# Paged attention in a decoder step: K and V pages laid on 64 partitions, and score and V products of 128 columns instead of 64

## What is computed

```python
k_past = cache_k[page_table].reshape(Bd, P, H, hd)
v_past = cache_v[page_table].reshape(Bd, P, H, hd)
s_past = jnp.einsum('bqhd,bkhd->bhqk', q, k_past) * FOX_SCALE
s_past = s_past + c_q - c_past.transpose(0, 2, 1)[:, :, None, :]
...                                # scores of the 8 new tokens, masked
p = jax.nn.softmax(jnp.concatenate([s_past, s_new], axis=-1), axis=-1)
o = einsum('bhqk,bkhd->bqhd', p[..., :P], v_past) + einsum('bhqk,bkhd->bqhd', p[..., P:], v_new)
```

## Time and profile before

| | |
|---|---|
| median of 3 runs | 1596.44 us (1595.81 to 1604.83) |
| profiled execution, own time | 1591.11 us |
| its span, first to last instruction | 1589.5 us |
| TensorE matmul / VectorE / ScalarE / GpSimd busy | 1444.3 / 727.8 / 563.9 / 530.6 us |
| mean granted TensorE clock | 0.973 |
| score products L1918, 4096 records | 75.7 us busy, 480.2 to 1201.8 us |
| V products L1952, 4096 records | 75.1 us busy, 545.4 to 1268.9 us |
| DMA | 250.51 MB, 153412 packets |

### The profile page before, as it was taken

How to read it: one execution, slowest core, us unless ns; L and a number is a source line. 1 busy time by engine, 2 the same in 40 slices (tenths; PEclk the granted TensorE clock), 3 DMA queues, 4 the chain that set the end, 5 groups by cost and what they waited for, 6 DMA issues and landing times. The chain is left out here.

```text
span 1589.5 us, 43485 instructions
## 1 busy us (share of the span) xinstructions
PE 1444.3 (91%) x16281; PEld 1224.5 (77%) x16281; DVE 727.8 (46%) x1578; ACT 563.9 (35%) x1311; POOL 530.6 (33%) x953
## 2 busy tenths in 40 slices
PE   5989899898978898899988999989898999999988
PEld 5878788787767776688877887769775798888876
DVE  4344353543636555655656555565354223333221
ACT  5343444343531334223452334423234364111100
POOL 4444434440056235344354524444241122111000
PEclk9999999999989999999999999989999999999999
DMA  5131312112248787899897999889975764331521
GB/s 173 32 75 44 85 41 76 41 49 68 55 130 221 194 231 202 229 239 226 237 261 201 267 232 251 219 213 249 209 197 156 225 249 136 109 102 62 166 93 60
DMA packets 153412, 250.51 MB, mean 158 GB/s; under 512 B 45898, under 2 KB 58827, under 8 KB 152691
## 3 DMA queue, kind: packets, MB, share of 16 engines
q1 hardware_dynamic: 121618, 215.68, 50.1%
q0 software_dynamic: 31584, 32.04, 7.3%
HBM read 217.37 MB, written 30.22 MB: 156 GB/s over the span
## 5 line engine op out<-in xcount | busy, mean ns | idle before, releaser
L289 PE MATMUL psum<-h_hi,w_hi 128*128 128x384 f32 (+1 forms) x1344 | 489.5, 364 | 11.7 <-issue 3.3
L289 PE MATMUL psum<-h_hi,w_lo 128*128 128x384 f32 (+1 forms) x1344 | 447.2, 333 | 0.0
L289 PE MATMUL psum<-h_lo,w_hi 128*128 128x384 f32 (+1 forms) x1344 | 446.3, 332 | 0.0
L1451 POOL DMA_DIRECT2D sc<-tmp_bias x512 | 279.3, 551 | 262.6 <-PE psum L1937 258.6
L289 PEld LDWEIGHTS psum<-h_hi,w_hi 128*128 128x128 f32 x1344 | 258.0, 192 | 61.5 <-issue 47.1
L289 PEld LDWEIGHTS psum<-h_lo,w_hi 128*128 128x128 f32 x1344 | 259.0, 193 | 2.3
L289 PEld LDWEIGHTS psum<-h_hi,w_lo 128*128 128x128 f32 x1344 | 258.0, 192 | 0.0
L674 POOL DMA_DIRECT2D lfp<-in_cache_logf x256 | 124.7, 487 | 176.2 <-issue 176.2
L1665 DVE STREAM_TRANSPOSE k_page<-k_page 128x1024 f32<-128x1024 f32 x128 | 156.1, 1232 | 28.4 <-DMA k_page<-in_cache_k 27.5
L264 DVE TENSOR_TENSOR w_lo<-w_raw,w_hi 128x1024 fp32r<-128x1024 f32 x63 | 76.9, 1220 | 109.5 <-ACT w_hi L259 109.2
L259 ACT ACTIVATE w_hi<-w_raw 128x1024 fp32r<-128x1024 f32 x63 | 66.1, 1049 | 59.5 <-DMA w_raw<-in_w_tiles 39.9
(11 more groups left out here) (259 smaller groups left out, 2164.4 us busy)
## 6 DMA issues: line engine op xcount, KB each, us to landing
k_page<-in_cache_k SPq DMA_DIRECT2D x256, 256.0 KB, 3.9
v_page<-in_cache_v SPq DMA_DIRECT2D x256, 256.0 KB, 4.9
w_raw<-in_w_tiles SPq DMA_DIRECT2D x63, 512.0 KB, 5.7
g_pair<-tmp_gates SPq DMA_DIRECT2D x16, 544.0 KB, 4.6
sc<-tmp_bias POOLq DMA_DIRECT2D x512, 16.0 KB, 4.5
tmp_ogla<-gate POOLq DMA_DIRECT2D x4, 1088.0 KB, 5.9
g_pair<-tmp_ogla SPq DMA_DIRECT2D x8, 544.0 KB, 7.6
x_in<-in_x_prompt SPq DMA_DIRECT2D x8, 512.0 KB, 6.2
```

The lines of the kernel that those rows point to most:

```text
L289: m = pe.matmul(out, wt[:, s, k, :], h[:, k, t0:t0 + w], start=(k == 0 and a == 0), stop=(k == KT_ - 1 and a == 2))
L1451: pool.dma_start(dst, src.unsqueeze(0).to_broadcast([TS, 2, 256])).then_inc(sc_in[j % SLOTS], 16)
```

## The change

K pages go to 64 partitions with two neighbouring tokens (4 KB, one piece in memory) on each; even pages of the new order take the lower half of the partitions and odd ones the upper half, and a slot holds two pages. `page_order` makes page 0, 16, 1, 17, ... of a sequence follow one another. V pages go to 64 partitions with two rows of 2 KB each; two pages lie in the lower half and two in the upper. The score product takes two slots side by side, 128 moving columns, and writes them with a step of two elements in PSUM, so that the tokens come out in order; where the two slots are the last and the first of the ring (13 sets of 64) it stays at 64 columns. The V product takes both heads of a pair in one product of 128 columns, of which each half of the 16 used rows keeps its own 64. The copies to `p_t` and `pn_t`, the pick in `od` and the stored order of the bias follow. No wait is added or removed.

```diff
@@ bias_store(g), SyncE, in the first half of the kernel
-rows = scratch["bias"][...].rearrange("h (q g t) -> q g h t", q=4, t=32)
+rows = scratch["bias"][...].rearrange("h (q g t) -> q g h t", q=4, t=HD)
-    sp.dma_start(rows[q], lfc[b * NPG:(b + 1) * NPG, :, 32 * q:32 * q + 32]).then_inc(b_stored, 16)
+    p0, t0 = b * NPG + q // 2 * (NPG // 2), q % 2 * HD
+    sp.dma_start(rows[q], lfc[p0:p0 + NPG // 2, :, t0:t0 + HD]).then_inc(b_stored, 16)
@@ tiles
-k_page = sb(ctx, "k_page", [P, NK, FW])
+k_page = sb(ctx, "k_page", [P, NK // 2, 2, FW])
-p_t = sb(ctx, "p_t", [P, 2, 2 * P + 24])
-pn_t = sb(ctx, "pn_t", [NSAMP + TS, 2, NHP, TS])[NSAMP:NSAMP + TS]
+p_t = sb(ctx, "p_t", [P, 2, 2 * P + 16])
+pn_t = sb(ctx, "pn_t", [NSAMP + TS, NHP, 2, TS])[NSAMP:NSAMP + TS]
@@ SyncE: page, load_k, load_v
-src = sp.value_load(pages[0:1, a:a + 1], ...)
+at = a // NPG * NPG + page_order(a % NPG)
+src = sp.value_load(pages[0:1, at:at + 1], ...)
-slot = a % NK
-sp.dma_start(k_page[:, slot, :], page("cache_k", a).rearrange("o p c -> (o p) c")).then_inc(k_in_page[slot // 2], 16)
+slot = a // 2 % (NK // 2)
+dst = k_page[rows[a % 2], slot]
+sp.dma_start(dst, page("cache_k", a).rearrange("o (i j) c -> (o i) j c", j=2)).then_inc(k_in_page[slot], 16)
-part, g = slice(a % 4 * 32, a % 4 * 32 + 32), a // 4 % 2
-sp.dma_start(v_page[part, g], page("cache_v", a).rearrange("o (b i) c -> (o i) b c", b=4)).then_inc(v_in_page[g], 16)
+dst, g = v_page[rows[a // 2 % 2], a // 4 % 2, a % 2 * 2:a % 2 * 2 + 2, :], a // 4 % 2
+sp.dma_start(dst, page("cache_v", a).rearrange("o (b i) c -> (o i) b c", b=2)).then_inc(v_in_page[g], 16)
@@ ScalarE: pstep, pn
-copied(p_t[:, g % 2, 0:2 * P], lift_bank("pt", s, g)[:, 0:2 * P])
+copied(p_t[:, g % 2, 0:2 * P].rearrange("p (x e q) -> p e x q", e=2, q=TS),
+       lift_bank("pt", s, g)[:, 0:2 * P].rearrange("p (e x q) -> p e x q", e=2, q=TS))
-copied(pn_t, rows32[:, :, :, 0:TS])
+copied(pn_t.rearrange("p h e q -> p e h q"), rows32[:, :, :, 0:TS])
@@ VectorE: kstep, od
-both = k_page[:, 2 * slot:2 * slot + 2, :].rearrange("p g c -> p (g c)")
+both = k_page[:, slot].rearrange("p j c -> p (j c)")
-    src = diag(lift_bank("od", s)[rows[half], 0:], 32, NHP)
+    src = diag(lift_bank("od", s)[rows[half], half * TS:], 32, NHP)
@@ TensorE: sstep (scores)
-for pair in range(2):
-    slot = (4 * (s * SETS + n) + 2 * pair) % NK
-    col = n % 2 * P + pair * HD
+slot = 2 * (s * SETS + n) % (NK // 2)
+runs = [(0, 2)] if slot + 2 <= NK // 2 else [(0, 1), (1, 1)]
+for first, width in runs:
+    at, col = (slot + first) % (NK // 2), n % 2 * P + first * HD
     for e in range(2):
         for f in range(2):
             for hp in range(NHP):
-                m = MM(bank[4 + e][32 * hp:32 * hp + 32, col:col + HD].rearrange("p (g t) -> p g t", g=2), q_row[:, b, :],
-                       k_page[:, slot:slot + 2, 32 * b:32 * b + 32], start=(f == 0), stop=(f == 1))
+                out = bank[4 + e][32 * hp:32 * hp + 32, col:col + width * HD].rearrange("p (g t j) -> p g j t", j=2, t=32)
+                m = MM(out, q_row[:, b, :], k_page[:, at:at + width, :, 32 * b:32 * b + 32], start=(f == 0), stop=(f == 1))
@@ TensorE: vstep (V products), pnv
-for tb in range(4):
-    for e in range(2):
-        for hp in range(NHP):
-            col = e * P + 32 * hp + TS * tb
-            h = 2 * hp + e
-            m = MM(bank[6][32 * hp:32 * hp + 32, e * HD:(e + 1) * HD], p_t[:, g % 2, col:col + 32], v_page[:, g % 2, tb, h * HD:(h + 1) * HD], ...)
+for r in range(4):
+    for hp in range(NHP):
+        col = 64 * hp + 2 * TS * r
+        m = MM(bank[6][32 * hp:32 * hp + 32, 0:P], p_t[:, g % 2, col:col + 32], v_page[:, g % 2, r, hp * P:(hp + 1) * P], ...)
-for e in range(2):
-    for hp in range(NHP):
-        h = 2 * hp + e
-        m = MM(bank[6][32 * hp:32 * hp + TS, e * HD:(e + 1) * HD], pn_t[:, e, hp, :], vn_raw[:, h * HD:(h + 1) * HD], ...)
+for hp in range(NHP):
+    m = MM(bank[6][32 * hp:32 * hp + 2 * TS, 0:P], pn_t[:, hp].rearrange("p e q -> p (e q)"), vn_raw[:, hp * P:(hp + 1) * P], ...)
@@ new helper
+def page_order(x):
+    return x % 2 * (NPG // 2) + x // 2
```

More of the change, by code:

```diff
@@ L635, in bias_store @@
                     for b in range(4):
-                        rows = scratch["bias"][(4 * g + b) * H:(4 * g + b + 1) * H, :].rearrange("h (q g t) -> q g h t", q=4, t=32)
+                        rows = scratch["bias"][(4 * g + b) * H:(4 * g + b + 1) * H, :].rearrange("h (q g t) -> q g h t", q=4, t=HD)
                         for q in range(4):
-                            sp.dma_start(rows[q], lfc[b * NPG:(b + 1) * NPG, :, 32 * q:32 * q + 32]).then_inc(b_stored, 16)
+                            p0, t0 = b * NPG + q // 2 * (NPG // 2), q % 2 * HD
+                            sp.dma_start(rows[q], lfc[p0:p0 + NPG // 2, :, t0:t0 + HD]).then_inc(b_stored, 16)
                 def end(i):
@@ L1391, in page @@
             def page(cache, a):
-                src = sp.value_load(pages[0:1, a:a + 1], min_val=0, max_val=NPHYS - 1)
+                at = a // NPG * NPG + page_order(a % NPG)
+                src = sp.value_load(pages[0:1, at:at + 1], min_val=0, max_val=NPHYS - 1)
                 return ins[cache][ds(src, 1)]
@@ L1523, in pstep @@
                 W(act, "pv", 0, s * SETS + g - 1)
-                copied(p_t[:, g % 2, 0:2 * P], lift_bank("pt", s, g)[:, 0:2 * P]).then_inc(lift_act, 1)
+                copied(p_t[:, g % 2, 0:2 * P].rearrange("p (x e q) -> p e x q", e=2, q=TS),
+                       lift_bank("pt", s, g)[:, 0:2 * P].rearrange("p (e x q) -> p e x q", e=2, q=TS)).then_inc(lift_act, 1)
             def exp(s):
@@ L1537, in pn @@
                 rows32 = lift_bank("pn", s)[0:TS, 0:2 * P].rearrange("p (e h c) -> p e h c", e=2, h=NHP)
[L1538 removed]
+                copied(pn_t.rearrange("p h e q -> p e h q"), rows32[:, :, :, 0:TS]).then_inc(lift_act, 1)
             def out(s):
@@ L1946, in vstep @@
                 stream.pass_waits(pe)
-                for tb in range(4):
-                    for e in range(2):
-                        for hp in range(NHP):
-                            col = e * P + 32 * hp + TS * tb
-                            h = 2 * hp + e
-                            m = MM(bank[6][32 * hp:32 * hp + 32, e * HD:(e + 1) * HD], p_t[:, g % 2, col:col + 32], v_page[:, g % 2, tb, h * HD:(h + 1) * HD],
-                                   start=(g == 0 and tb == 0 and e == 0), stop=(g == SETS - 1 and tb == 3 and e == 1), skip_group_check=True)
+                for r in range(4):
+                    for hp in range(NHP):
+                        col = 64 * hp + 2 * TS * r
+                        m = MM(bank[6][32 * hp:32 * hp + 32, 0:P], p_t[:, g % 2, col:col + 32], v_page[:, g % 2, r, hp * P:(hp + 1) * P],
+                               start=(g == 0 and r == 0), stop=(g == SETS - 1 and r == 3))
                 inc(m, "pv")
@@ L1968, in pnv @@
                 stream.pass_waits(pe)
-                for e in range(2):
-                    for hp in range(NHP):
-                        h = 2 * hp + e
-                        m = MM(bank[6][32 * hp:32 * hp + TS, e * HD:(e + 1) * HD], pn_t[:, e, hp, :], vn_raw[:, h * HD:(h + 1) * HD],
-                               start=False, stop=False, skip_group_check=True)
+                for hp in range(NHP):
+                    m = MM(bank[6][32 * hp:32 * hp + 2 * TS, 0:P], pn_t[:, hp].rearrange("p e q -> p (e q)"), vn_raw[:, hp * P:(hp + 1) * P],
+                           start=False, stop=False, skip_group_check=True)
                 inc(m, "pvn")
```

1 line of the change is left out of this document (removed).

## The result

| | before | after |
|---|---|---|
| median of the runs, us | 1600.26 (4 runs, 1595.81 to 1604.83) | 1619.20 (4 runs, 1611.73 to 1621.79) |
| profiled execution, us: own time, span | 1591.11, 1589.5 | 1620.05, 1618.4 |
| mean granted clock | 0.973 | 0.963 |

The ratio is 1.0122, with a 95% interval of 1.0083 to 1.0161: the change makes the kernel 19 us slower. The two profiled executions differ by 29 us, more than the medians, so of their differences only the large ones count.

A forecast was written before the change was run, and what follows sets the result against it. The prediction took TensorE and the DMA engines as both almost full from 700 to 1200 us; K transfers added 43 us, all else 0, so 1591.11 + 43 = 1634 us profiled, median 1640 us, range 1583 to 1685 us.

The forecast's parts named there:

- The part bound by transfers, and K as the cause: Page loads, 700 to 1200 us: DMA-bound, K on 64 partitions costs the engines more; main case, chance 0.46.
- Two of the forecast's signs: If right: fewer than 160 K pages from 700 to 1200 us, and L1918 to the end at about 1245 us.
- the engine work of a set: DMA work of a set's page loads, 700 to 1200 us: from 11.2 to 12.84 us, +1.64 us from four K pages.
- the 43 us made of it: 700 to 1200 us: 12.84 us at share 0.97 is 13.24 against 12.2 us, +1.04 us x 41 sets.
- the middle of the two rows: K page on 64 partitions priced at 156 ns per 2 KB, between 146 and 165: 1.25 us against 0.84.
- V at 0: V page loads, 32 to 64 partitions with the same 2 KB packets: no change, at best -0.6 us a set.
- The formula for the full part: 700 to 1200 us: DMA work of a set divided by 0.97, the best share seen, sets the time once over 12.2 us.
- Before and after these stretches there is room: Outside 500 to 1200 us no loss, share 0.66 from 1200 to 1300; 500 to 700 us also priced at 0.
- SyncE "not changed, not the bound": Issue of page loads on SyncE: as many loads, 1.05 us each, 8.4 us in a set of 12.2; no cost.
- Products at 0: TensorE's wider V and score products: +5 to -6 us, taken as 0; groups of 32 records at 1.05 to 1.14 us.
- The step of two in PSUM: Rival: stepped score writes run at half speed, 56 us over 64 sets, 1652 or about 1657 us; chance 0.14.
- Both halves at once (cancelled or faster): Rivals: K pages on opposite halves load side by side; cancelled 1590 to 1602 us, chance 0.22; faster 1574 us, 0.18.

The follow-up runs named there:

- wide_k64: The changed kernel with V pages loaded as before (32 partitions in a row) and K still on a half; ratio 1.0105 to the kernel before.
- narrow_both64: The kernel before, keeping its 64-column products, with both page loads of the changed kernel (K and V on halves); ratio 1.0177.
- narrow_reads: The kernel before with three more unused page-number reads a set on SyncE; ratio 1.0002.
- wide_fixed: The changed kernel without page-number reads on SyncE, loading page a instead of the page the table names; ratio 1.0046 to the kernel before.
- k_step2_right_one: The kernel before with K pages on every second partition, 128-column V products and 64-column score products written in token order by an output step; ratio 1.0004.
- wide_v64: The changed kernel with K pages loaded as before (128 partitions) and V still on a half; ratio 0.9970 to the kernel before.

## Why the forecast had the sign and not the size

**The part bound by transfers, and K as the cause: right.** K pages cost the engines more, both landings rose to 5.5 us, the DMA share passed 0.95 and the waits for `k_page` grew from 8.6 to 37.8 us. Taking K off its half took the loss away. The change's transfers alone, without SyncE's limit, cost 1.07%, some 17 of the 19 us. Two of the forecast's signs did not come, both because the loss is smaller: the list from 700 to 1200 us has 163 K pages, not fewer than 160, and the scores end at 1223.1 us, not at 1245.

**The term that was mis-sized: the engine work of a set, and the 43 us made of it.** The forecast added +1.64 us (K +0.41 us a page, V 0). A set carries 97.28 MB / 41 = 2.37 MB on this queue, nine times 256 KB. By the table that is 9 x (1.11 - 1.03) = +0.7 us; with K alone on its half it is 9 x (1.15 - 1.03) = +1.1 us. K's +0.30 us a page, read from the K pages alone (1.14 - 0.84), lies just under the lower end that the forecast had taken from the stores of the earlier trace rows, so the middle of the two rows was the wrong choice. In other kernels with K on a half the same reading gives 1.05 us (`wide_k64`) to 1.19 (`narrow_both64`), so the 1.25 us of the forecast lies above all of them. V at 0 holds: a V page takes 1.36 us in the changed kernel against 1.32, and at an equal pace of issue half of the partitions costs what a quarter does. The -0.5 us that V alone shows in the table, 9 x (0.97 - 1.03), need not be a gain of the 64 partitions: `narrow_reads` shows the same with V as before and only SyncE slower, and that SyncE stays as it is was a premise of the forecast.

**The formula for the full part: too sharp, with too low a ceiling.** The forecast divided by 0.97 as the best share seen in 50 us. From 870 to 920 us the kernel before stands at 1.04, and `wide_fixed` at 1.00 over 500 us:

```profile
870.00:920.00 50.00, 48.53 (x861) 43.01 (x860) 30.18 (x55) 20.72 (x53) 28.20 (x52) 1.00 1.04 262
```

With a ceiling of 1.00 the same +1.64 us gives 12.84 us a set, 0.64 x 41 = +26 us instead of +43. With 0.97 and the measured work it gives +3 us at +0.7 us a set ((11.2 + 0.7) / 0.97 = 12.27 us) and +24 us at four times K's +0.30 us. Measured, this stretch lost 12 to 13 us. A rule that knows only full or not full turns half a microsecond of work in a set into 21 us of time. The trace shows something softer: at 0.96 on the mean VectorE waited 16 times for K pages, at 0.92 it did so 9 times.

**"Before and after these stretches there is room": wrong for the start.** The forecast's 0 from 500 to 700 us holds from 587 us on. But 11 us were lost between 460 and 587 us, where ten K pages, eight V pages and the next K pages follow each other closely, and where the DMA share was 0.90 (460 to 480 us) and 0.86 (480 to 500 us) in the kernel before already. So the nearness of any sum to the 19 us would be luck in part: 12 to 13 us stand against the 43 of the full stretch, and some 8 to 15 us come from places where the forecast had nothing. For sizing, the runs with room on SyncE give a slope: 0.85, 1.03, 1.15 us of engine time give 0.991, 0.998, 1.011, so 0.4% and then 1.0% of the time for each 0.1 us, each ratio with an interval of 0.3 to 0.5% to both sides.

**SyncE "not changed, not the bound": wrong in the first half, and the second holds only as long as the engines are full.** Its instructions are 1.76 us a set longer. In the change itself no run shows a cost of this beyond some tenths of a per cent (1.0122, against 1.0107 without reads). But it is why stepped partitions for K and V bring the change to 1.0009 instead of 0.99: a gain of the transfers goes as far as SyncE's room and stops.

**Products at 0: right.** 1.08 and 1.10 us a group, inside 1.05 to 1.14. All else equal the times differ by 0.2% and 0.5%, within the intervals. The mean granted clock of the profiled executions is 0.963 against 0.973; other executions of the kernel before have 0.960 to 0.978, so nothing can be read from that.

**The step of two in PSUM: the rival falls.** 272 against 273 ns a record, and 1.10 us for the group of 64. Of the Trainium skill's "Advanced Engine Details and Errata", PSUM Cachelines, the rule that any other pattern than pairs slows a matmul is not borne out here for fp32 columns at this pace. `k_step2_right_one` even writes its columns 32 ahead and 30 back in turn, and its groups of 64 records take 1.10 us too:

```profile
705.05 1.10 PE L1922 MATMUL psum<-k_page,q_row 128*32 128x64 f32 x64
```

**Both halves at once (cancelled or faster): falls.** In the change even and odd pages alternate between the halves and still pay. What does work is a transfer whose partitions lie on a stride through both halves. The Trainium skill's "SBUF — State Buffer", section on Door 1, finds the port from the partition's number, and by that formula every second or every fourth partition of the whole buffer reaches all 16 ports, while 64 neighbours reach 8; with the runs this agrees (0.86 against 1.14 us for a K page). The conclusion of that section of the Trainium skill that 64 in a row do no better than 32 agrees with the runs at an equal pace of issue: 1.16 us in `wide_v64` (1.24 from 482 to 488 us) and 1.16 in `narrow_reads` (1.20 from 476 to 484 us). In the changed kernel, where such pages follow K pages on a half, they took 1.36 us (87.6% x 6 / 1.01 x 0.262); that fits a page that costs more the more crowded the engines are, but this was not tested by itself.

**Open.** Whether a version that keeps the function can be faster than the kernel before. V pages on stepped partitions need the probabilities in the same order, and the bias is stored in token order in runs of 32; I found no order that serves both and tried none. Nor was a second queue for the loads tried, which would give SyncE room. And that exactly K's longer instruction, not its layout, holds the stepped version is inferred from kernels that lose alike as SyncE's room shrinks (73 us with one read, 56 us with K stepped) and from the runs without reads, not from one where K's instruction alone is changed.

## What to carry to other kernels

Price a transfer by which partitions it covers, not by how many: 32 or 64 on a stride through the whole buffer cost what 128 do (0.84 to 0.87 us for 256 KB), 32 or 64 neighbours 1.05 to 1.36 us, more where the loads follow each other more closely. Then read the issuing engine's own waits as a second resource, since an edit that halves the partitions of a load can also lengthen its instruction. And when a suspected cost shows nothing in one kernel, that only says that there is room for it there: the three reads that were free in the kernel before, with 165 us of room, cost 3.1% in a kernel with faster transfers and 94 us of room. Last, look at the dense start of a stretch by itself; its mean share says little about the first 100 us.

## What the runs showed of the hardware that was not expected

- The DMA instruction on SyncE takes 333 to 338 ns for one row of 2 KB on 128 partitions and 322 to 337 ns for 32 partitions in a row with four blocks, but 469 to 492 ns for 64 partitions of 4 KB and 599 to 636 ns for 64 partitions of two blocks. On every fourth partition the same four blocks take 602 to 633 ns. So neither the count of partitions nor that of the rows sets it alone (medians of the runs with page-number reads, 500 to 1200 us). Nor does the transfer alone: the same weight load takes 432 ns in the kernel before and 593 in the changed one.
- A K page on 64 neighbouring partitions takes 1.14 us of the engines, on every second one 0.86 us, with the same rows. A V page on 32 neighbours takes 1.32 us, and 1.16 when the same loads are issued a third further apart; on every second or fourth partition it takes 0.85 to 0.86 us.
- Matmul records that write PSUM with a step of two, or 32 ahead and 30 back in turn, take as long as others: 1.10 us for 64 records of 64 columns.
